# The order of two token halves in every odd eighth of a projection

## What is computed

```python
for i in range(2):
    h = rmsnorm(x, norm_mix_pre[i])
    proj = h @ (w_in_attn if i == 0 else w_in_ssm)           # input projection
    a = attention(proj) if i == 0 else ssm_mixer(proj)
    c = cross_attend(cq, mem_k[i], mem_v[i])
    x = x + rmsnorm(concat([a, c]) @ w_out[i], norm_mix_post[i])   # output projection
    h = rmsnorm(x, norm_ffn_pre[i])
    f = square(relu(h @ w_up[i])) @ w_down[i]                # 4096 wide
    x = x + rmsnorm(f, norm_ffn_post[i])
```

## Time and profile before

| | |
|---|---|
| median of three runs | 1782.18 us (1780.83 to 1782.9) |
| profiled execution, own time | 1780.53 us |
| profiled execution, span | 1778.7 us |
| mean granted TensorE clock | 0.991 |
| PE busy | 1684.8 us, 95% of the span |
| DVE, ACT, POOL busy | 65%, 47%, 33% |

### The profile page before, as it was taken

The page is one execution under the profiler, slowest core; times in us unless marked ns, Lnnn a source line. Parts: engine busy times, 40 slices in busy tenths (PEclk is TensorE's granted clock), DMA queues, the critical chain, the costliest instruction groups (busy, mean ns, idle before and its releaser), DMA issues. The chain is left out here.

```text
span 1778.7 us, 31700 instructions
## 1 busy us (share of the span) xinstructions
PE 1684.8 (95%) x12611; PEld 1609.3 (90%) x12611; DVE 1155.3 (65%) x2100; ACT 836.0 (47%) x1606; POOL 579.0 (33%) x361
## 2 busy tenths in 40 slices
PE   6999999999999999999999999989999999999996
PEld 5987877998999999998899999987998899999996
DVE  6437777315774838477879797957306774838477
ACT  6426666324433434345455666555424534434342
POOL 1231211241443343432135344440341353343431
PEclk9999999999999999999999999999999999999998
DMA  6621121121322312221223222331221222313221
GB/s 224 210 72 58 58 66 31 60 84 48 106 84 72 105 64 105 72 102 54 76 81 106 91 95 90 107 102 56 72 84 43 100 84 80 111 60 107 70 97 54
DMA packets 51491, 153.11 MB, mean 86 GB/s; under 512 B 12400, under 2 KB 14160, under 8 KB 51088
## 3 DMA queue, kind: packets, MB, share of 16 engines
q1 hardware_dynamic: 43968, 139.99, 22.9%
q10 hardware_dynamic: 7376, 11.10, 2.0%
HBM read 144.16 MB, written 6.47 MB: 85 GB/s over the span
## 5 line engine op out<-in xcount | busy, mean ns | idle before, releaser
L1189 PE MATMUL ps<-big_hi,w_hi 128*128 128x288 f32 x2528 | 559.4, 301 | 12.0 <-POOL w_lo L2411 4.7
L1189 PE MATMUL ps<-big_lo,w_hi 128*128 128x288 f32 x2528 | 540.1, 297 | 7.4 <-DVE big_lo L1665 7.2
L1189 PE MATMUL ps<-big_hi,w_lo 128*128 128x288 f32 x2528 | 544.5, 295 | 0.0
L2411 POOL TENSOR_TENSOR w_lo<-raw,w_hi 128x1024 fp32r<-128x1024 f32 x116 | 283.5, 2445 | 682.3 <-ACT w_hi L611 572.9
L1189 PEld LDWEIGHTS ps<-big_hi,w_hi 128*128 128x128 f32 x2528 | 408.8, 189 | 20.8 <-issue 13.1
L1189 PEld LDWEIGHTS ps<-big_lo,w_hi 128*128 128x128 f32 x2528 | 402.1, 189 | 12.7 <-DVE big_lo L1665 11.8
L1189 PEld LDWEIGHTS ps<-big_hi,w_lo 128*128 128x128 f32 x2528 | 407.8, 189 | 0.1
L1479 PE MATMUL ps<-col_hi,w_hi 128*128 128x288 f32 x896 | 267.6, 299 | 19.0 <-DVE mix L2058 18.3
L1479 PE MATMUL ps<-col_hi,e_lo 128*128 128x288 f32 x896 | 264.4, 295 | 0.0
L1479 PE MATMUL ps<-col_lo,w_hi 128*128 128x288 f32 x896 | 264.1, 295 | 0.0
L611 ACT ACTIVATE w_hi<-raw 128x1024 fp32r<-128x1024 f32 x176 | 185.7, 1055 | 153.6 <-DMA raw<-in_slabs 88.7
(11 more groups left out here) (223 smaller groups left out, 2285.7 us busy)
## 6 DMA issues: line engine op xcount, KB each, us to landing
raw<-in_slabs SPq DMA_DIRECT2D x238, 512.0 KB, 3.3
row<-acs_prompt ACTq DMA_DIRECT2D x16, 384.0 KB, 4.0
bias<-in_alibi SPq DMA_DIRECT2D x12, 256.0 KB, 2.7
x<-in_x SPq DMA_DIRECT2D x2, 1152.0 KB, 8.5
out_h<-state ACTq DMA_DIRECT2D x4, 384.0 KB, 2.6
out_y<-x SPq DMA_DIRECT2D x2, 576.0 KB, 2.8
raw<-in_slabs SPq DMA_DIRECT2D x4, 256.0 KB, 3.8
kms<-in_mk SPq DMA_DIRECT2D x2, 512.0 KB, 5.2
```

What stands on the lines that cost most here:

```text
L1189: ins = pe.matmul(ps[:, bank + h, 0:hi_c - lo_c], weight(w, s, kt), a[:, k0 + kt, lo_c:hi_c], start=start, stop=stop, skip_group_check=True)
L2411: pool.tensor_tensor(w_lo[:, s % RING], raw[:, s % RING], w_hi[:, hi_place(s)].bitcast(F32), ALU.subtract).then_inc(lo_done, 1)
```

## The change

In an odd eighth (kt = 1, 3, 5, 7) the two halves swap places. The three pairs, the operands, the banks, the waits and the increments stay.

```diff
             def eighth(s, g, kt, hi, lo, k0=0, cols=TOK, start=True, stop=True, tile=None):
 
 
-                both = range(2 if cols == TOK else 1)
-                for w, a, order in ((w_hi, hi, both), (w_lo, hi, reversed(both)), (w_hi, lo, both)):
+                both = (0, 1) if cols == TOK else (0,)
+                if kt % 2:
+                    both = both[::-1]
+                for w, a, order in ((w_hi, hi, both), (w_lo, hi, both[::-1]), (w_hi, lo, both)):
                     if tile is not None and w is w_hi:
```

## The result

The changed kernel takes 1790.49 us (median of six, 1789.02 to 1797.61), against 1782.1 us before. The medians are 8.4 us apart, and the ratio is 1.0056, with a 95% interval of 1.0043 to 1.0068, about 10 us: slower, where no change was forecast and 1787 was the upper end. The profiled execution took 1789.02 us, 8.5 us more than the one before.

A forecast was written before the change was run, and what follows sets the result against it. PE's matmul pace was taken as the bound. Gains of 0.31 us and losses of 0.37 summed to a 0.06 us loss, taken as 0 on the 1782.2 median, or 1782.0 with a small seam allowance; range 1776.5 to 1787.

The forecast's parts named there:

- What bounds the kernel: Whole kernel: PE, busy 95% of the span, sets the time by its matmul pace; readers wait for PE.
- The parts costed at nothing: Moved `slab_done` increment, readers' and ring reload's start, `start` flag, `freed` wait, first bank: all as before, 0 us.
- The two paces: Dense stretches of L1189: the same six instructions take 790 or 800 ns per eighth, for a reason the rows don't tell.
- K and V: First dense stretch of L1189: 24.00 us, taken at 133.3 ns per matmul, the slow pace.
- What is a change of half worth?: At 1192 seams, one change of half fewer: 0.5 ns gained or 0.65 lost each; bounds 2.4 us gained, 2.7 lost.
- neither costs a step: Rival 4, the forecast: the half sets only the moving operand's address and the bank, worth nothing; under 0.2% either way, chance 0.53.
- Rival 3: Output projections and layer 1's input: 576 fast eighths fall to the slow pace, 5.8 us lost, 1787.9; chance 0.19.
- The gap of the formula: Matmul steps of 131.7 and 133.3 ns exceed the estimated 122.5 by 9 to 11; order effects can hide only there.

The follow-up runs named there:

- e4: Kernel before with halves 0,1,0,1,0,1 in every eighth, six changes and none kept: 1778.29 us, ratio 0.9974.
- e7: Kernel before with halves 0,1,1,0,1,0 in even eighths and 1,0,0,1,0,1 in odd ones: 1777.63 us, ratio 0.9969.
- e1: Kernel before with halves 1,0,0,1,1,0 in every eighth, half and tile still changing together at the seam: 1776.53 us, ratio 0.9969.
- e6: Kernel before with halves 0,1,1,0,1,0 in every eighth, the half kept at every seam without alternation: 1776.53 us, ratio 0.9971.
- e8: Kernel before with the eighths' matmuls reading one half's activations into both banks, in two runs: half 0 alone 1773.03 us, half 1 alone 1786.49.
- e3: Kernel before with only the PSUM banks swapped in odd eighths, activations read in the old order: 1784.73 us, ratio 1.0009.
- e10: Changed kernel with half 1's reads begun 32 columns earlier, 1024 bytes behind half 0: 1772.94 us, one execution.
- e15: Changed kernel with half 1's reads begun 64 columns earlier, 896 bytes behind half 0: 1791.92 us, one execution.
- e16: Changed kernel with half 1's reads begun 16 columns earlier, 1088 bytes behind half 0: 1775.97 us, one execution.
- e2: Kernel before with only the activations swapped in odd eighths, PSUM banks in the old order: 1794.39 us, ratio 1.0056.
- e17: Kernel before, order unchanged, with half 1's reads begun 32 columns earlier, 1024 bytes behind half 0: 1777.68 us, ratio 0.9973.
- e14: Kernel before, unchanged, profiled once more on another chip: 1789.6 us, both output projections at 800 ns per eighth.
- e18: Changed kernel with tokens split 256 and 320 instead of 288 and 288 for kt = 1 to 7: 1778.10 us, ratio 0.9981 against the kernel before.
- e9: Kernel before with halves 0,1,0,1,0,1 in the ffn's up projections and 1,0,0,1,1,0 elsewhere: 1771.65 us, ratio 0.9950.

## Why the prediction was wrong

**What bounds the kernel: right.** PE's pace set the time. The stretches that are bound by it fell behind by 8.7 us in a profile that is 8.5 us longer, and the readers waited for PE longer than before, DVE 106.2 us in place of 103.9. The parts costed at nothing (increment, readers, reload) cost nothing that shows.

**The two paces: read rightly, and then left aside.** The prediction saw 790 and 800 ns for the same instructions and said that it could not tell what picks one. (The stretch that it calls K and V, at 800 ns, is that of the four query slabs; the three slabs of K and V, 73 to 92 us, went at 790. That moves its sum by less than 0.1 us.) It went on to price the order by other streams, as though the pace were a sum of steps.

**The step that failed: "What is a change of half worth?"** It took four changes of half against none, divided by four, and found 0.5 and -0.65 ns, so 0 in sum, with bounds of 2.4 us gained and 2.7 lost. There is no price per change of half: the term was put at 0 with 2.7 us lost as its bound, and measured 8 to 10 us lost. Orders with six, five and four changes (e4, e7, e1 and e6) all ran at 780 to 800 ns, and the changed one with three at 800 to 806. What the neighbouring streams also hid is that they read at places of their own. The first part of L1172 in the earlier trace rows, 132.1 ns, is not "one half throughout": it has the 24 matmuls of half 0 and six of half 1. The second, 133.1 ns, is half 1 alone. Parted rightly, six steps of half 0 come to about 791 ns and six of half 1 to 799, near the 790 and 800 that e8 shows for the halves. The rows had the cause in them, and were taken for the width of an unknown.

**The premise of the forecast, "neither costs a step": half right.** The bank costs nothing (e3). The moving operand's address does (e8, e10, e15, e16). With half 1 an odd multiple of 128 bytes behind half 0, the pace depends on the order of the reads; with 1024 or 1088 bytes the new order has one pace, and with 1024 so has the old one.

**Rival 3 was the right one, and its range too short.** It had the slow pace take over the stretches that were fast, 5.8 us at most, and that happened in full: 1.2 us in each output projection and 3.4 in layer 1's input. But the slow stretches had a slower pace still, 806 ns, which no row of before shows. The ffn at +6 ns (2.2 us) and the second output projection at 806 in place of 800 (0.7 us) are what took the time past the end of the range. The range held that 800 ns was the slowest that an eighth could be, since it was the slowest seen.

**The gap of the formula.** The prediction said of the section "Back-to-back issue gap" of the page "TensorE: Matmul & The Clock Gate" of the Trainium skill that an effect of order can hide only in what its estimate of 122.5 ns leaves out. The runs fit that: the fastest mean step seen is 780 / 6 = 130.0 ns, the slowest 134.3. What the prediction drew from the section "Step-by-step: what each phase is for" of that page of the Trainium skill, that the order is worth nothing because load and stream have read ports of their own, does not hold for this stream: 1.0056, by the activations' order alone (e2). Whether the ports are as the section says no run here shows.

**What stays open.** Which order gives which pace is not explained: an odd multiple of 128 bytes allows 780 ns (e4, e6) as well as 806, and the well placed e10, e16 and e17 had 790 in the stretches shown, never 780. That it is the odd multiple of 128 that does it rests on two slow distances, 896 and 1152 bytes, against 1024 and 1088. What selects among an order's paces when a stretch begins was not found, only that it can differ between two executions of one program (e14). Nor was it followed what decides where the clock falls for 3.4 us, at 1.5 us or so each time, which is what parts the profiled executions of e17 and e18 from that of e10 at nearly the same pace. The place counts in a stream that reads one half alone (e8, L1172); whether by itself or by its relation to the weight tile that loads meanwhile was not tried. And e9's order was chosen from one profile of each order.

## What to carry to other kernels

In a kernel bound by a dense stream of matmuls, look at where the moving operands begin before arranging their order: a start at an odd multiple of 128 bytes made the order matter by 3% of an eighth, a start at 1024 bytes made it worth nothing between the two orders tried. Count matmuls in a fixed stretch of the profile: the pace showed in one look what single times, spread over 9 us, could not. And where two traces have the same instructions, set start against start: it parts the pace from what the clock did elsewhere. Two paces for the same instructions mean an unexplained cause, and a range must then allow a third.

## What was not expected of the hardware

- An eighth, six matmuls of 288 columns with their weight loads, takes 780, 790, 800 or 806 ns in the mean of a long stretch, and stretches of one pace agree to within 0.1%, at a granted clock of 1.00 throughout. Single eighths can differ much more, in a fixed pattern: 787 and 793 ns in turn in the output projections of before, 800 each time in its ffn, 785 to 837 where the mean is 806.
- The same matmuls reading only half 0 take 790, only half 1, 1152 bytes on, 800 ns, per eighth.
- In e4 the 800 ns are not spread evenly. The pairs in an output projection are 0.26, 0.27, 0.26, 0.27 us apart, every second one longer, across the borders of the eighths:

```profile
340.22 0.42 PE L1189 MATMUL ps<-big_lo,w_hi 128*128 128x288 f32 x2
340.48 0.43 PE L1189 MATMUL ps<-big_hi,w_hi 128*128 128x288 f32 x2
340.75 0.42 PE L1189 MATMUL ps<-big_hi,w_lo 128*128 128x288 f32 x2
341.01 0.43 PE L1189 MATMUL ps<-big_lo,w_hi 128*128 128x288 f32 x2
341.28 0.42 PE L1189 MATMUL ps<-big_hi,w_hi 128*128 128x288 f32 x2
```

So something recurs every fourth matmul, not every sixth; what it is no run here shows.
